# Expert weights loaded in 16 KB runs per partition, with the contraction order regrouped

## What is computed

```python
def expert_choice_ffn(h, w_router, w_gate, w_up, w_down):
    cap = EC_CAPACITY * N // N_EXPERTS                     # 32 tokens per expert and request
    aff = jax.nn.softmax((h @ w_router).astype(jnp.float32), axis=-1)
    gates, idx = lax.top_k(aff.T, cap)
    xe = h[idx]
    hid = jax.nn.silu(jnp.einsum('ecd,edf->ecf', xe, w_gate)) * jnp.einsum('ecd,edf->ecf', xe, w_up)
    ye = jnp.einsum('ecf,efd->ecd', hid, w_down) * gates[..., None]
    return jnp.zeros_like(h).at[idx.reshape(-1)].add(ye.reshape(-1, D))
```

## Time and profile before

| | |
|---|---|
| median of three runs | 1770.5 us (1769.29 to 1770.71) |
| span of the profiled execution | 1768.4 us; the page gives no other time for it |
| PE, weight loads, DVE, ACT, POOL busy | 94%, 52%, 28%, 20%, 1% |
| DMA packets | 162406, 479.78 MB |
| HBM read, written | 473.85 MB, 6.03 MB |
| loads of expert weights | 192 of 2048 KB |

### The profile page before, as it was taken

The page is one execution under the profiler, slowest core; times in us unless marked ns, Lnnn a source line. Parts: engine busy times, 40 slices in busy tenths (PEclk is TensorE's granted clock), DMA queues, the critical chain, the costliest instruction groups (busy, mean ns, idle before and its releaser), DMA issues.

```text
span 1768.4 us, 18647 instructions
## 1 busy us (share of the span) xinstructions
PE 1659.4 (94%) x7790; PEld 919.3 (52%) x7790; DVE 495.1 (28%) x728; ACT 353.0 (20%) x552; POOL 23.5 (1%) x23
## 2 busy tenths in 40 slices
PE   8999999999999999989999898898998998988987
PEld 7888887788876787863333232332332232222322
DVE  3433325544873432331011021120120110111202
ACT  5422224523454432220000000000000000000000
POOL 1100000000000000000100000000000000000000
PEclk9999999999999999999999999999999999999999
DMA  8433331233210443188999999999999999999997
GB/s 295 117 96 95 107 95 48 84 84 95 75 45 1 171 173 108 48 322 319 410 409 409 409 410 410 410 410 410 409 410 410 409 410 410 410 410 410 409 409 284
DMA packets 162406, 479.78 MB, mean 271 GB/s; under 512 B 20112, under 2 KB 32528, under 8 KB 162352
## 3 DMA queue, kind: packets, MB, share of 16 engines
q1 hardware_dynamic: 161280, 476.23, 70.2%
q0 software_dynamic: 1072, 2.77, 0.7%
HBM read 473.85 MB, written 6.03 MB: 271 GB/s over the span
## 4 chain that ended last, share of the span: by engine, by line
PE 73%; DMA 18%; SPq 4%; DVE 3%; ACT 1%; issue 1%; DVEq 0%; ACTq 0%
PE ps L1458 16%; PE ps L1245 11%; PE ps L1247 11%; PE ps L1246 11%; DMA ring<-w_up 8%; DMA ring<-w_gate 8%; PE ps L1430 7%; PE ps L1443 6%; SPq L546 4%; PE ps L1311 2%; PE ps L1293 2%; PE ps L1408 2%; DMA ring<-w_down 1%; PE ps L1333 1%; PE ps L1321 1%
## 5 line engine op out<-in xcount | busy, mean ns | idle before, releaser
L1458 PE MATMUL ps<-ring,xeT 128*64 128x512 f32 x1968 | 445.4, 597 | 61.2 <-DMA ring<-w_up 40.0
L1458 PEld LDWEIGHTS ps<-ring,xeT 128*64 128x64 f32 x1968 | 133.9, 137 | 364.2 <-issue 267.7
L1443 PE MATMUL ps<-ring,hidT 128*64 128x512 f32 x1008 | 221.5, 594 | 6.3 <-DMA ring<-w_down 5.6
L1245 PE MATMUL ps<-w_hi,actT_hi 128*128 128x512 f32 x512 | 200.3, 391 | 1.7 <-DVE w_lo L901 1.4
L1247 PE MATMUL ps<-w_hi,actT_lo 128*128 128x512 f32 x512 | 199.4, 389 | 0.0
L1246 PE MATMUL ps<-w_lo,actT_hi 128*128 128x512 f32 x512 | 199.2, 389 | 0.0
L901 DVE TENSOR_TENSOR w_lo<-w_raw,w_hi 128x2048 fp32r<-128x2048 f32 (+1 forms) x56 | 126.2, 2254 | 213.6 <-ACT w_hi L692 213.6
L1157 DVE TENSOR_TENSOR y<-y,ps 128x1024 f32<-128x1024 f32 x64 | 78.2, 1221 | 371.8 <-PE ps L1430 371.8
L1443 PEld LDWEIGHTS ps<-ring,hidT 128*64 128x64 f32 x1008 | 70.3, 137 | 146.6 <-issue 131.9
L692 ACT ACTIVATE w_hi<-w_raw 128x2048 fp32r<-128x2048 f32 (+1 forms) x57 | 106.5, 1868 | 196.3 <-PE ps L1247 192.2
L855 ACT ACTIVATE hid<-ps 128x512 f32<-128x512 f32 x16 | 9.6, 597 | 596.2 <-PE ps L1458 596.2
(11 more groups left out here) (213 smaller groups left out, 1451.0 us busy)
## 6 DMA issues: line engine op xcount, KB each, us to landing
ring<-w_gate SPq DMA_DIRECT2D x63, 2048.0 KB, 22.9
ring<-w_down SPq DMA_DIRECT2D x63, 2048.0 KB, 23.8
ring<-w_up SPq DMA_DIRECT2D x60, 2048.0 KB, 23.5
w_raw<-w_in SPq DMA_DIRECT2D x31, 1024.0 KB, 5.3
w_raw<-w_out SPq DMA_DIRECT2D x16, 1024.0 KB, 5.1
extra<-w_up SPq DMA_DIRECT2D x4, 2048.0 KB, 13.8
w_raw<-w_kv_up SPq DMA_DIRECT2D x16, 256.0 KB, 3.9
w_raw<-w_q_up SPq DMA_DIRECT2D x12, 256.0 KB, 4.2
```

The lines of the kernel that those rows point to most:

```text
L1245: pe.matmul(out, a_hi, hi[:, k, :], start=kk == 0, stop=False)
L1443: mm = pe.matmul(ps[64 * n:64 * n + 64, 2 + h, :], hidT[:, k, 64 * a:64 * a + 64], w[:, k, 512 * n:512 * n + 512], start=a == 0 and k == 0 ...
L1458: mm = pe.matmul(ps[64 * half:64 * half + 64, m // 4, :], xeT[:, b, c, 64 * n:64 * n + 64], w[:, c, 512 * half:512 * half + 512], start=m ...
```

## The change

Each partition now gets neighbouring rows, so that a piece is one run of 16 KB per partition. In a gate or up piece, partition p holds rows 4p to 4p+3 of the 512. A down piece is now 256 whole rows of 8 KB, two neighbouring ones per partition. The contraction index of chunk c is therefore 4p+c (2p+c for down) instead of 128c+p, and the other operand is regrouped to match: ACT and DVE read PSUM at a step of 4 elements (xe) or 2 (hid) and write the groups one behind the other. xeT takes its gain from a second copy of g2 in the new order, 16 more columns of constants. A down piece gives all 2048 output columns from a quarter of the rows, so all four parts of ye are complete only after piece 11: ACT waits for it ahead of the first part, PE waits for all four parts of the expert before, ahead of piece 8, and the last eight scatter rounds come after piece 11. mla_max shares an address with a tile used later.

```diff
             def load_piece(e, i):
                 dst, landed, _ = place(e, i)
                 w = (w_gate, w_up, w_down)[i // 4]
-                if i < 8:
-                    src = w[e].rearrange("(q c p) n -> q p c n", q=4, p=P)[i % 4]
-                    dst = dst[:, :].rearrange("p (c n) -> p c n", c=4)
-                else:
-                    src = w[e].rearrange("(a k p) (h n) -> h a p k n", a=2, h=2, p=P)[i // 2 % 2, i % 2]
-                    dst = dst[:, :].rearrange("p (k n) -> p k n", n=1024)
-                sp.dma_start(dst, src).then_inc(landed, 16)
+                src = w[e].rearrange("(q p c) n -> q p (c n)", q=4, p=P)[i % 4]
+                sp.dma_start(dst[:, :], src).then_inc(landed, 16)
...
+        def of_runs(row, c):
+            return row.rearrange("p (b r c) -> p b c r", c=c, r=P)
+        def in_runs(row, c):
+            return row.rearrange("p (b c r) -> p b c r", c=c, r=P)
...
-                act.activation(xe[:, 0, :], ps[:, 4, :], ACT.Copy).then_inc(xe_act, 1)
+                act.activation(in_runs(xe[:, 0, :], 4), of_runs(ps[:, 4, :], 4), ACT.Copy).then_inc(xe_act, 1)
...
-                act.activation(hid[:, :], ps[:, 0, :], ACT.Silu).then_inc(silu_ready, 1)
+                act.activation(in_runs(hid[:, :], 2), of_runs(ps[:, 0, :], 2), ACT.Silu).then_inc(silu_ready, 1)
...
+                act.wait_ge(piece_used, 12 * e + 12)
                 for h in range(2):
-                    act.wait_ge(piece_used, 12 * e + 10 + 2 * h)
                     for n in range(2):
...
-                dve.tensor_copy(xe[:, 1, :], ps[:, 5, :]).then_inc(xe_dve, 1)
+                dve.tensor_copy(in_runs(xe[:, 1, :], 4), of_runs(ps[:, 5, :], 4)).then_inc(xe_dve, 1)
...
-                    gain = cc("g2", 8 * b, 8).rearrange("p (n c) -> p c n", n=2).unsqueeze(3)\
+                    gain = cc("g2_runs", 8 * b, 8).rearrange("p (n c) -> p c n", n=2).unsqueeze(3)\
...
-                dve.tensor_tensor(hid[:, :], hid[:, :], ps[:, 1, :], ALU.mult).then_inc(hid_ready, 1)
+                dve.tensor_tensor(in_runs(hid[:, :], 2), in_runs(hid[:, :], 2), of_runs(ps[:, 1, :], 2), ALU.mult)\
+                   .then_inc(hid_ready, 1)
...
             def down(e, i, first):
-                h, a = (i - 8) // 2, i % 2
-                w = landed(e, i)[:, :].rearrange("p (k n) -> p k n", n=1024)
+                a = i - 8
+                w = landed(e, i)[:, :].rearrange("p (k n) -> p k n", n=D)
                 if a == 0 and not first:
-                    pe.wait_ge(ye_ready, 4 * e + 2 * h - 2)
-                for k in range(4):
-                    for n in range(2):
-                        mm = pe.matmul(ps[64 * n:64 * n + 64, 2 + h, :], hidT[:, k, 64 * a:64 * a + 64],
-                                       w[:, k, 512 * n:512 * n + 512], start=a == 0 and k == 0, stop=a == 1 and k == 3)
+                    pe.wait_ge(ye_ready, 4 * e)
+                for k in range(2):
+                    for h in range(2):
+                        for n in range(2):
+                            mm = pe.matmul(ps[64 * n:64 * n + 64, 2 + h, :],
+                                           hidT[:, 2 * (a % 2) + k, 64 * (a // 2):64 * (a // 2) + 64],
+                                           w[:, k, 1024 * h + 512 * n:1024 * h + 512 * n + 512],
+                                           start=a == 0 and k == 0, stop=a == 3 and k == 1)
...
                 for m in range(8, 12):
                     down(e, m, first)
-                    if not more and m % 2:
-                        last_rounds(m - 9)
-                        last_rounds(m - 8)
+                if not more:
+                    for q in range(4):
+                        last_rounds(q)
```

More of the change, by code:

```diff
@@ L55 @@
 for _name, _n in [("ident", P), ("g1", KD), ("g_naq", 1), ("g_nak", 1), ("g_qa", 4), ("g_kva", 4), ("g_qn", 1),
-                  ("g_kn", 1), ("g_mix", KD), ("g2", KD), ("wr", KD * 32), ("iota", SLOTS),
+                  ("g_kn", 1), ("g_mix", KD), ("g2", KD), ("g2_runs", KD), ("wr", KD * 32), ("iota", SLOTS),
                   ("fold64", ROPE), ("fold16", EXPERTS), ("cos", 2 * ROPE), ("sin", 2 * ROPE),
@@ L176, in hybrid_layer @@
     rden = small("rden", [P, 32, 2])
+    mla_max = at("mla_max", [P, 16, 2], TOP[0])
     pick1h = small("pick1h", [P, 2, 2, SLOTS])
@@ L184, in hybrid_layer @@
             small("ssum_h", [P, NT, 4]), small("ssum_proj", [P, 32])]
-    mla_max = small("mla_max", [P, 16, 2])
     assert TOP[0] <= 229344, TOP[0]
@@ L1544, in constants @@
                  g_mix=np.concatenate([column("na_out_norm"), column("mla_out_norm")], 1), g2=column("norm2_g"),
+                 g2_runs=np.asarray(inputs["norm2_g"])[0].reshape(4, P, 4).transpose(1, 0, 2).reshape(P, KD),
                  wr=wr.reshape(P, -1), fold64=np.tile(np.eye(ROPE), (2, 1)),
```

## The result

The changed kernel takes 1731.2 us (median of four runs, 1730.2 to 1731.8) against 1770.4 us before: a ratio of 0.978, 95% interval 0.977 to 0.979, 39 us faster. The forecast was 1773 us and no measurable difference; its range began at 1752. It missed.

A forecast was written before the change was run, and what follows sets the result against it. The prediction took the DMA engines' expert stream, 5.12 us per piece, as the bound. Terms 0 + 0 + 0 + 2.5 us gave 1770.9 us in the profile and 1773.0 us as a median, range 1752 to 1780.

The forecast's parts named there:

- What bounds the kernel: Whole expert stream: the DMA engines set 5.12 us per piece at 409 or 410 GB/s; a per cent of rate is worth 9.4 us.
- The loads: All 192 pieces, from 4 KB to 16 KB runs: rate of 16 KB packets taken as unchanged, 0 us.
- the slow side: Worst end of the price of the loads: at 387 GB/s a piece takes 5.42 us, 55 us more in all.
- Strided reads: PSUM reads by ACT and DVE at steps of 2 or 4 elements: bound 0 to 0.7 us, taken as 0.
- The down pieces: Down product with same shapes, new order, ACT waiting for the fourth piece before its ye copies: costs nothing.
- The tail: Last expert: all eight scatter rounds now stand behind piece 11, 2.5 us more.
- A: Loads: fixed cost per packet also at 4 KB, 4.1 ns, 0.098 us per piece, 18 us less: 1755; chance 17%.
- B: Loads: the straight line through 512 B and 2 KB holds, 57 us less, 1716; chance 7%.
- C: Loads: stream gets slower as engines read further apart in HBM; at 387 GB/s 55 us more, 1828; chance 11%.

## Why the prediction was wrong, step by step

**What bounds the kernel: right.** The expert stream at a fixed rate from 801 us to its end, SP always ahead of it, PE waiting 1.4 us per piece. That a per cent of rate is worth 9.4 us held nearly: 4.4% less time per piece is 41.2 us, and 40.5 came. In the steady stretch PE did not become the bound, since a pair takes 117.5 us and PE needs 111. In the third expert it did for a moment (the 342 GB/s above), which the forecast did not look for.

**The loads: this step failed.** "So there is a cost of 4.1 ns that shows at 512 B, and it is gone at 2 KB." Measured: 9.3 ns per packet at every size from 2 to 16 KB, 24 packets fewer per piece and engine, 0.224 us per piece and 41 us on 184. The forecast had the right rows and chose between them wrongly. It called all its rows those of a saturated queue. But it set a 2 KB rate from 2 us of a load that stood alone beside a 4 KB rate from 44 us of a stream, and found them equal. Its 512 B row is a short load too (SP's timeline has it as w_q_up, not w_kv_up): in slices of 0.2 us from 410 to 418 us the rate stands above 300 for some 1.4 us and then falls,

```profile
GB/s 0 0 0 0 0 0 0 0 59 82 56 151 328 335 333 343 348 341 297 205 228 200 184 253 289 320 282 182 159 138 97 33 0 0 0 0 0 0 0 0
```

Both short loads lie some 4 ns under the line of the long streams: 80.0 against 84.6 ns at 2 KB, 24.1 against 28.1 at 512 B. The forecast put the one 2 KB row of a queue that stays full, 387 GB/s, down to what is read and priced the slow side with it. That row, with the 410 of 4 KB, is the line: 84.7 and 160.0 ns give 75.3 ns for 2048 bytes, 27.2 bytes per ns, and 9.4 ns per packet; for 16 KB 612 ns and 4.90 us per piece. The answer stood in rows 7 and 10; that the 387 was the packet and not what is read, only the runs with 2 KB packets of expert weights could settle.

**Strided reads: right**, at the good end of the bound. No row showed them before; the groups after do, at 0.60 and 0.69 us. The Trainium skill ("SBUF — State Buffer", section on the DMA port swizzle) says that PSUM has lines of 8 bytes and that reads or writes of it that are not contiguous slow matmuls down. That this also holds for reads by ACT and DVE was the forecast's reading, and these rows do not bear it out: 597 ns at a step of 16 bytes, as for one of 4. What the page says of matmuls no run here tried.

**The down pieces: right**, nothing. **The tail: right in mechanism and size**, 2.5 us forecast, 2.3 between the two profiles.

**The rivals.** A had the mechanism, a fixed cost per packet also at 4 KB, and 17%; its size was taken from a 512 B row and came out at 4.1 ns instead of 9.3. B's line, 57 us, went through the two short loads: its slope, 27.5 bytes per ns, is nearly right, and its 5.5 ns per packet is 4 too small, as both its points are. The truth lay between A and B, below the low end of the range. The Trainium skill ("DMA: Bandwidth & Descriptors", section "Why small descriptors are slow") has the right sign: a fixed cost per packet. Its 3 cycles would give 1.7%, an estimate by that page, and the runs show 4.4% less time, 2.6 times as much. The section "Where 436 GB/s comes from" of the same page gives a ceiling of 435 GB/s; the slope found here, 27.2 bytes per ns on sixteen engines, is 435 GB/s. C's mechanism is refuted for distance. With the loads at 4 KB again, the forecast's own number came out: 1773.2 us. So its other terms stand, and the one at zero was the error.

## What to carry to other kernels

In a stream that the DMA engines bound, count packets as well as bytes: here, from HBM into SBUF, a packet cost an engine some 9.3 ns beside its bytes at 27.2 bytes per ns, so 4 KB runs leave 6% of the rate unused and 16 KB runs 1.5%; the way to long runs is to give a partition neighbouring rows and to regroup the other operand where it is copied anyway. Take the price of a packet from two queues that stay full, never from a short load beside a long one. A faster stream can meet an engine that gives its buffers back late: look at the busiest iteration too. A reorder made for the loads can take work out of a gap elsewhere: look at the last iteration by itself.

## What the runs showed of the hardware that was not expected

- After an idle stretch, 2 KB packets from rows 128 apart go at 408 GB/s for some 2.5 us, are at 391 in the next 2 us, and settle at 387. Out of one 16 KB stretch they start at 392 and settle at 387 too. The profiles show the rates, not the reason.
- ACT and DVE read float32 from PSUM at steps of 8 and 16 bytes in the time of a dense read (597, 684 and 691 ns for 512 elements).
- Short loads of 2 KB packets from rows 8 KB apart on the same partition climb more slowly than from rows 128 apart (5.7 against 5.1 us to landing, one profile of 16 loads), while 16 KB runs move at 428 GB/s whether neighbours lie 16 or 64 KB apart. Why is open.
- The granted clock just ahead of the first expert differs between executions: 0.72 from 797 to 800 us in the profile before, 1.00 in the profile after. The same gather took 5.34 and 3.64 us.
